# Three later attentions: factors multiplied on GpSimd, turned probabilities moved by VectorE and ScalarE

## What is computed

```
def _masked_softmax(s, mask):
    s = jnp.where(mask, s.astype(jnp.float32), NEG_INF)
    p = jnp.where(mask, jnp.exp(s - jnp.max(s, axis=-1, keepdims=True)), 0.0)
    return p / jnp.maximum(jnp.sum(p, axis=-1, keepdims=True), 1e-30)
...
        pr = jax.nn.softmax(sc.astype(jnp.float32), axis=-1).astype(v.dtype)
        return jnp.einsum('bkgqs,bskd->bqkgd', pr, v)
```

## Time and profile before

| | us |
|---|---|
| median of three runs | 2258.02 (2257.19, 2258.02, 2265.61) |
| span of the profiled execution, first to last instruction | 2259.1 |
| nsa attention, about | 591 to 663 (72) |
| mla attention, about | 1079 to 1100 (21) |
| gqa attention, about | 1691.5 to 1724.5 (33) |

### The profile page before, as it was taken

How to read it: one execution, slowest core, us unless ns; L and a number is a source line. 1 busy time by engine, 2 the same in 40 slices (tenths; PEclk the granted TensorE clock), 3 DMA queues, 4 the chain that set the end, 5 groups by cost and what they waited for, 6 DMA issues and landing times.

```text
span 2259.1 us, 30958 instructions
## 1 busy us (share of the span) xinstructions
PE 1817.0 (80%) x13243; PEld 1133.4 (50%) x13243; DVE 430.9 (19%) x1014; ACT 396.2 (18%) x898; POOL 0.6 (0%) x5
## 2 busy tenths in 40 slices
PE   7989898899898999899997556656799975666655
PEld 5858655558666655577764121211477641222113
DVE  2232311113443111032321000000134210000001
ACT  2030211111442111132321000000214210000001
POOL 0000000000000000000000000000000000000000
PEclk9999799999899999999998887777999997776868
DMA  9866599985644999953479999999933699999994
GB/s 358 251 252 237 201 384 400 409 264 153 234 177 172 373 370 390 370 170 107 173 272 413 422 421 421 421 422 421 373 125 140 259 414 421 421 422 421 422 422 184
DMA packets 184735, 716.11 MB, mean 317 GB/s; under 512 B 28396, under 2 KB 95896, under 8 KB 114072
## 3 DMA queue, kind: packets, MB, share of 16 engines
q1 hardware_dynamic: 183884, 713.61, 80.8%
q10 hardware_dynamic: 716, 0.53, 0.1%
HBM read 826.30 MB, written 1.05 MB: 366 GB/s over the span
## 4 chain that ended last, share of the span: by engine, by line
PE 54%; DMA 35%; DVE 5%; SPq 3%; ACT 2%; issue 2%; ACTq 0%; DVEq 0%
DMA ring<-in_w 27%; PE ps L985 19%; PE ps L1416 7%; DMA ring<-in_moe_w_up 7%; PE ps L1336 5%; PE ps L1428 3%; PE ps L1322 2%; PE ps L1346 2%; PE ps L1363 2%; PE ps L962 2%; PE ps L1139 2%; SPq L807 1%; DMA ring<-in_ada_w 1%; SPq L869 1%; PE ps L999 1%
## 5 line engine op out<-in xcount | busy, mean ns | idle before, releaser
L1416 PE MATMUL ps<-ring,ptb 128*32 128x512 f32 x1936 | 317.5, 806 | 201.0 <-DMA ring<-in_w 187.6
L1416 PEld LDWEIGHTS ps<-ring,ptb 128*32 128x32 f32 x1936 | 83.4, 141 | 422.9 <-issue 407.9
L1428 PE MATMUL ps<-ring,pb 128*32 128x512 f32 x1024 | 153.4, 756 | 89.0 <-DMA ring<-in_w 86.4
L985 PE MATMUL ps<-xT,ring 128*128 128x256 f32 (+2 forms) x640 | 146.7, 389 | 1.0 <-ACT xT L1720 0.4
L1428 PEld LDWEIGHTS ps<-ring,pb 128*32 128x32 f32 x1024 | 41.2, 134 | 195.1 <-issue 191.1
L985 PEld LDWEIGHTS ps<-xT,ring 128*128 128x128 f32 (+2 forms) x640 | 117.9, 187 | 29.1 <-issue 8.4
L985 PE MATMUL ps<-oT,ring 128*128 128x256 f32 x512 | 114.0, 382 | 2.0 <-DVE oT L2228 1.1
L2456 DVE TENSOR_TENSOR kT<-pb,ps 128x1024 f32<-128x1024 f32 x8 | 9.8, 1222 | 531.8 <-ACT pb L1894 531.8
L985 PE MATMUL ps<-hT,ring 128*128 128x256 f32 x480 | 109.0, 386 | 1.3 <-ACT hT L1720 1.3
L1336 PE MATMUL ps<-ring,yT 128*32 128x256 f32 x1536 | 91.1, 395 | 18.2 <-DMA ring<-in_moe_w_up 17.2
L1336 PE MATMUL ps<-ring,vt 128*32 128x256 f32 x1536 | 93.3, 401 | 14.8 <-DMA ring<-in_moe_w_up 13.7
(11 more groups left out here) (437 smaller groups left out, 1955.3 us busy)
## 6 DMA issues: line engine op xcount, KB each, us to landing
ring<-in_w SPq DMA_DIRECT2D x370, 1024.0 KB
ring<-in_moe_w_gate SPq DMA_DIRECT2D x96, 1024.0 KB
ring<-in_moe_w_up SPq DMA_DIRECT2D x96, 1024.0 KB
ring<-in_moe_w_down SPq DMA_DIRECT2D x96, 1024.0 KB
ring<-in_ada_w SPq DMA_DIRECT2D x48, 1024.0 KB
ring<-in_diff_w_in SPq DMA_DIRECT2D x12, 1024.0 KB
ring<-in_w_o SPq DMA_DIRECT2D x8, 1024.0 KB
ring<-in_ple_gate_w SPq DMA_DIRECT2D x8, 1024.0 KB
```

The costliest lines, as they stand in the source:

```text
L985: last = mmul(o, l, r, start=start, stop=stop)
L1416: last = mmul(ps[32 * j:32 * j + 32, 2 * a + h, :], xg[:, k, 32 * j:32 * j + 32], w[j][2 * k2 + h], start=(k == 0), stop=(k == C - 1))
L1428: last = mmul(ps[32 * j:32 * j + 32, 6 + h, :], hidT2[:, c, 32 * j:32 * j + 32], w[j][2 * c2 + h], start=(c == 0), stop=(c == C - 1))
```

## The change

In nsa, mla and gqa (not in diff) the multiplication of the probabilities moves from VectorE to GpSimd, as four `tensor_scalar` instructions a step, one for each head and query half, in place. VectorE only makes the four factors of a row and signals `coef_ready`. The move of the turned probabilities is split: ScalarE moves bank 6 (first head), VectorE bank 7 (second head, `move_high`, new semaphore `pt_high`). In these attentions VectorE's `outputs(i-2)` now stands ahead of `neg_max(i+2)`. TensorE waits for `pt_high` as well, before `transposes` and before `values`. Two semaphores, `vbd_ready` and `ada_add`, give way to waits of VectorE on its own chain.

```
@@ TensorE, transposes
                         if n >= 1:
                             pe.wait_ge(S("pt_ready"), n)
+                        if shared_no(x):
+                            pe.wait_ge(S("pt_high"), shared_no(x))
@@ TensorE, values
                     pe.wait_ge(S("pt_ready"), n + 1)
+                    if x["kind"] != "diff":
+                        pe.wait_ge(S("pt_high"), shared_no(x) + 1)
@@ ScalarE, move
                     elif x["causal"]:
-                        last = func(pt[:, :, 0:384], ps[:, 6:8, 0:384], ACT.Copy)
+                        last = func(pt[:, 0, 0:384], ps[:, 6, 0:384], ACT.Copy)
                     else:
-                        last = func(pt, ps[:, 6:8, :], ACT.Copy)
+                        last = func(pt[:, 0, :], ps[:, 6, :], ACT.Copy)
@@ VectorE, normalise
-                        for tt, cols in enumerate((slice(0, P), slice(P, P + T)) if x["causal"] else
-                                                  (slice(0, T), slice(T, 2 * T))):
-                            w = cols.stop - cols.start
-                            rb = r[:, 2 * tt:2 * tt + 2].rearrange("p (u o) -> p u o", o=1).to_broadcast([P, 2, w])
-                            last = V.tensor_tensor(p[:, :, cols], p[:, :, cols], rb, ALU.mult)
+                        last.then_inc(S("coef_ready"), 1)
+                        return
                     last.then_inc(S("p_ready"), 1)
+
+                def move_high(x):
+                    n, pt = x["n"], pt_of(x)
+                    dve.wait_ge(S("t_done"), n + 1)
+                    dve.wait_ge(S("v_done"), n - 1)
+                    cols = slice(0, 384 if x["causal"] else 512)
+                    V.tensor_copy(pt[:, 1, cols], ps[:, 7, cols]).then_inc(S("pt_high"), 1)
@@ VectorE, loop of the three attentions
+                        if i >= 2:
+                            outputs(xs[i - 2])
+                        if i + 2 < len(xs):
+                            neg_max(xs[i + 2])
+                        move_high(x)
@@ GpSimd
+            def weigh(x):
+                p, r = p_of(x), stat(x, "coef")
+                pool.wait_ge(S("coef_ready"), shared_no(x) + 1)
+                for tt, cols in enumerate((slice(0, P), slice(P, P + T)) if x["causal"] else
+                                          (slice(0, T), slice(T, 2 * T))):
+                    for u in range(2):
+                        a = 2 * tt + u
+                        last = nc.gpsimd.tensor_scalar(p[:, u, cols], p[:, u, cols], r[:, a:a + 1], None, ALU.mult)
+                last.then_inc(S("p_ready"), 1)
```

More of the change, by code:

```diff
@@ L718, in program, with shared_no @@
         st_span = {k: [x for x in steps if x["kind"] == k] for k in ("diff", "nsa", "mla", "gqa")}
+        def shared_no(x):
+            return x["n"] - len(st_span["diff"])
         o_after, outs = {}, 0
@@ L2204, in normalise @@
                     dve.wait_ge(S("exp_done"), x["n"] + 1)
-                    link(V.reciprocal(r, stat(x, "sum")))
+                    last = V.reciprocal(r, stat(x, "sum"))
                     if x["kind"] == "diff":
+                        link(last)
                         link(V.tensor_tensor(r[:, 1:4:2], r[:, 1:4:2], coef[:, 0:2], ALU.mult))
@@ L2215, in normalise @@
                         if x["coef"] is not None:
+                            link(last)
                             r3 = r.rearrange("p (t u) -> p t u", t=TT)
-                            link(V.tensor_tensor(r3, r3, x["coef"], ALU.mult))
-                        for tt, cols in enumerate((slice(0, P), slice(P, P + T)) if x["causal"] else
-                                                  (slice(0, T), slice(T, 2 * T))):
-                            w = cols.stop - cols.start
-                            rb = r[:, 2 * tt:2 * tt + 2].rearrange("p (u o) -> p u o", o=1).to_broadcast([P, 2, w])
-                            last = V.tensor_tensor(p[:, :, cols], p[:, :, cols], rb, ALU.mult)
-                    last.then_inc(S("p_ready"), 1)
+                            last = V.tensor_tensor(r3, r3, x["coef"], ALU.mult)
+                        last.then_inc(S("coef_ready"), 1)
+                        return
+                    last.then_inc(S("p_ready"), 1)
+                def move_high(x):
[4 more added lines that the diff above has]
+                    V.tensor_copy(pt[:, 1, cols], ps[:, 7, cols]).then_inc(S("pt_high"), 1)
                 def outputs(x):
@@ L2233, in attention @@
                     normalise(x)
[L2234 to L2237, removed]
+                    if name == "diff":
+                        if i + 2 < len(xs):
+                            neg_max(xs[i + 2])
+                        if i >= 2:
+                            outputs(xs[i - 2])
+                    else:
+                        if i >= 2:
+                            outputs(xs[i - 2])
+                        if i + 2 < len(xs):
+                            neg_max(xs[i + 2])
+                        move_high(x)
                 for x in xs[-2:]:
@@ L2645, in _ @@
                 last = V.tensor_tensor(vbd[:, g, :, :], vbd[:, g, :, :], bd, ALU.mult)
-            last.then_inc(S("vbd_ready"), 1)
+            link(last)
             dve.wait_ge(S("vt_ready"), 1)
@@ L2695, in _ @@
             nc.gpsimd.memset(rowsA[:, :, :], 0.0).then_inc(S("rows_zero"), 1)
+            def weigh(x):
[7 more added lines that the diff above has]
+                last.then_inc(S("p_ready"), 1)
+            for name in ("nsa", "mla", "gqa"):
+                for x in st_span[name]:
+                    weigh(x)
 _INS = ["x", "c", "positions", "ada_w", "ada_b", "norm_g", "final_g", "diff_w_in", "diff_w_out", "diff_lambda",
```

1 line of the change is left out of this document (removed).

## The result

The changed kernel takes 2324.08 us (2320.89 to 2328.28, 4 runs) against 2261.82 (2257.19 to 2265.76, 4 runs) of the kernel before: +62.3 us, ratio 1.0277 with a 95% interval of 1.0258 to 1.0297. The prediction said 2264.4 in a range of 2257 to 2284; the change is slower, and by far more than any rival had been given. The profiled execution's span is 2326.5 against 2259.1, +67.4. Measured from the memset or copy that starts an attention to its last output, the three attentions (nsa, mla, gqa) take 100.69, 35.0 and 58.5 us instead of 72.0, 22.23 and 33.05: +66.9. So the whole loss lies inside them, as the prediction's frame says; only its size is another.

A forecast was written before the change was run, and what follows sets the result against it. TensorE's 3.2 us of work was taken as about a whole gqa step, with the new ring of waits setting a floor; gqa +2.2, mla +1.1 and nsa +3.1 on 2258.0 gave 2264.4 us, range 2257 to 2284.

The forecast's parts named there:

- the prediction's frame: Time lost or won inside the attentions is not made up by DMA (0.01 busy in gqa) and reaches the end in full.
- the price of GpSimd's product: In each step, GpSimd's product was taken at VectorE's 0.347 us for 256 columns and 0.286 for 128.
- The bracket: Limits set for GpSimd's product of 256 columns: GpSimd's MEMSET, 0.31, below and ScalarE's product, 0.59, above.
- B: Rival: in every step GpSimd multiplies slower than VectorE did, over 0.415 for 256 columns; 2283.5 at ScalarE's price; chance 0.29.
- B2: Rival: GpSimd's products take twice VectorE's time in every step, 0.69 and 0.57; 2293.7 us; chance 0.07.
- the sum: Changes of the three attentions added up: gqa +2.2, mla +1.1, nsa +3.1, in all +6.4 us.
- the modulations: After nsa's three modulation parts on TensorE, values wait for ScalarE's move, 0.31 shorter: -0.9 us.
- Rival D: Idle time in the steps keeps TensorE at half clock: steps about 6.2, +20 in gqa, some 2283; chance 0.03.
- the ring: Waits through GpSimd's products, transposes, VectorE's copy and next reciprocal; a step at least 3.38 in gqa and mla, 3.11 in nsa.
- rival C: Freed engines shorten the attentions' steps, with four GpSimd products (P) at 0.94; 2256.5 us; chance 0.05.
- rival E: The split move's halves run one behind the other if ScalarE's came late; costs nothing, kept in the forecast without own chance.
- the hand-over from VectorE to GpSimd: In each step, the time from VectorE's reciprocal to the next engine's start, taken as 0.20 us.

## Why the prediction was wrong

**What failed: the price of GpSimd's product.** The step "I take that one: it is the same instruction and near the row of the engine itself" put VectorE's 0.347 and 0.286 in the place of 0.922 and 0.602. The same instruction on another engine is another price, and the engine's own row, MEMSET, holds no arithmetic. The bracket failed with it: its upper end, 0.59, was ScalarE's price, not a bound on GpSimd at all. The slope told against B ("0.83 ns a column is under VectorE's 1.04") was a slope of writing. So B and even B2, at 0.69, stopped short, though B's sign, a product over 0.42, is what the rows show. The Trainium skill, GPSIMD Engine Reference, "Engine selection", on which the prediction drew against B2, puts one input at about line rate; 0.922 does not agree with that here, nor does the order of the two kinds: the product of two tensors (0.722) is cheaper than that of one tensor by a factor.

**With the price put right, the sum holds.** gqa: seven steps of 5.61 and 0.88 for the first are 40.15 against 22.07, +18.1; behind the last reciprocal 3.62 - 1.29 - 0.33 = +2.0. mla: 3 x 5.61 - 8.85 = +8.0, and +2.0. nsa with 4.82: four short intervals +2.34, the last +3.18, six long ones about +1.28, the modulations -0.9: +19.3. Together +49.4. The attentions of the kernel that keeps the clock up are 59.1 longer than before. Of the 9.7 that the sum lacks, 6.2 are in nsa's modulation intervals and the first intervals of nsa and mla (8.21, 6.49 and 7.38, where the changed kernel mostly has 7.34, 5.57 and 5.81, without idle products), and 1.3 in nsa's end, for which the sum has no term. So it holds to about a sixth; that the time of that kernel, +49.6, is almost the same number is chance.

**Rival D** was right in its cause and wrong in its price and its chance. The prediction argued that the ring would leave TensorE busy "3.2 of 3.4"; in a ring of 5.6 it is not, and the clock was at 0.50 in about half of the steps. But a slow step costs 0.87, not 2.8: of TensorE's work only the transposes lie on the ring (1.98 for 1.11), scores and values run beside GpSimd. It was treated as a case of its own, though it hangs on the price: over gqa the granted clock is 0.84 to 0.87 in the kernels here with products on GpSimd and steps of up to 4.1, 0.78 at steps of 4.4 and 0.72 at those of the changed kernel. (Its 6.2 a step is also short of twice 3.2; and rival C's P of 0.94 does not follow from 0.347, from which three times 0.1 less is 1.09. Neither enters the sum of the forecast.)

**What held.** Time lost in the attentions reached the end in full in the profiled executions (+66.9 of +67.4). The ring's formula, in kernels with four prices of the product, came within 0.07 us of the steps at full clock. The copies cost 0.692 and 0.558. The moves run side by side (rival E did not occur). Two of nsa's three modulation intervals got 0.25 shorter (7.34), where 0.3 was taken; the third met the half clock and took 8.28. The part of the ring that was assumed and is off is the hand-over from VectorE to GpSimd, 0.27 (1768.97 to 1769.24) instead of 0.20, which is what the formula lacks.

**What the expectations missed.** Three times GpSimd's own time was expected to be the limit, and each time another ring of two steps was: 10.15, 8.82, then 7.96 us for two steps. The second ring was there before the change and had not been added up. Its products and the maximum, in the chain of the kernel before in gqa, and the products of the last version, with shared products and the old order:

```profile
1704.17 1.30 DVE hT L2222 x2
...
1708.74 1.23 DVE mx L2198
...
1710.61 1.30 DVE hT L2222 x2
```

```profile
1702.07 2.00 POOL hT L2715 x2
...
1709.26 2.00 POOL hT L2715 x2
```

Before, two steps take 1710.61 - 1704.17 = 6.44, hardly more than twice TensorE's 3.2, so a longer product had no room. With products of 2.00, and 0.06 more from the reciprocal to GpSimd's start, the same ring is 6.44 + 0.70 + 0.06 = 7.20; measured are 7.19, the 3.6 a step against 3.15 that the last expectation missed. With 3.63 it is 8.83, and the products alone measured 8.82.

## What to carry to other kernels

Price an operation by a row of the same engine doing the same arithmetic; where there is none, the neighbours' rows are guesses and no bounds, and the chance should sit with the dear side when the operation lies on a ring that every step goes round. Measure such a price alone first: one short list on scratch told here the price on which the forecast failed. And write the ring down as a sum of rows: it stays right when a price in it changes, tells what the next price would give, and when it is opened the next longest ring must be looked for in the same way.

## What the runs showed of the hardware

- GpSimd multiplies float32 by a factor a row at 2.5 ns a column (0.447, 0.602, 0.922 and 1.562 for 64, 128, 256 and 512); by a tensor at 2.1 (0.452, 0.722, 1.263 for 128, 256, 512); by a broadcast factor in the two-tensor form at 1.7 (0.614 and 1.041 for 256 and 512). It copies at 0.83.
- Some VectorE instructions grow while GpSimd multiplies: the product of four columns for the bias takes 0.21 to 0.45 in eight steps of the changed kernel, each time beside a product of GpSimd, and 0.17 in the others; products of 256 columns take 0.461 on average for 0.347. The Trainium skill, SBUF — State Buffer, "SBUF: two separate sides", tells of a port pair that the two share and that an instruction of GpSimd, or one of VectorE of certain kinds, holds for its whole length while the other waits. The trace agrees that they hinder each other, but VectorE's products grew by 0.11 on average (the longest took 0.572), not by a whole product of 0.922.
- The granted clock was at 0.50 in about half of the steps of the attentions where TensorE waited some 2 to 4 us in each step for GpSimd, and at 0.99 in gqa when idle products filled the wait.
